# A two-layer hybrid encoder step: scores of head pairs in separate PSUM banks, layers written out, weights through 20 stages

## The reference

```
h = rms_norm(x, norm_g)
proj = h @ w_in                       # bq bf | bi bg | cq ck | cv cg | iq | ak av ik iw | aq | ag
# HGRN2, per chunk:  att = (q exp(b)) (k exp(-b))^T, causal;  o = att v + (q exp(b)) S
# retention:         att = q k^T * decay;                     o = att v + (q R) * scale
out = x + concat(ya, yb, yc) @ w_out
```

## Time and profile before

| | us |
|---|---|
| median of 3 runs | 4273.15 (4270.22 to 4276.17) |
| profiled execution | 4272.64, span 4271.0 |
| PE busy | 3742.6 (88%) |
| DVE busy | 2621.5 (61%) |
| ACT busy | 2346.7 (55%) |
| POOL busy | 991.2 (23%) |

### The profile page before, as it was taken

One profiled execution on the slowest core, in us unless ns is written; L12 is line 12 of the kernel. 1 busy time (PEld: TensorE's weight loads), 2 busy tenths in 40 slices (PEclk: granted clock), 3 DMA queues, 4 the chain that ended last, 5 costly groups with the idle time before them and its releaser, 6 DMA issues. The chain is left out here.

```text
span 4271.0 us, 57610 instructions
## 1 busy us (share of the span) xinstructions
PE 3742.6 (88%) x17620; PEld 1778.7 (42%) x17620; DVE 2621.5 (61%) x6004; ACT 2346.7 (55%) x4386; POOL 991.2 (23%) x1712
## 2 busy tenths in 40 slices
PE   3899999996788889989939999999967888899897
PEld 1555555552233333243315555555522333332433
DVE  4666666665666767566356666666656767676562
ACT  4333333333788888877343333333247888888772
POOL 0000000002643332333100000000026433323330
PEclk9899999997799899989969999999977998999899
DMA  6211111114310000010151111111142110000010
GB/s 208 69 36 35 36 34 35 37 34 113 94 43 29 20 22 20 23 33 29 39 160 51 35 35 35 35 35 35 29 122 83 45 34 10 22 30 17 29 34 36
DMA packets 168675, 202.94 MB, mean 48 GB/s; under 512 B 76592, under 2 KB 114480, under 8 KB 168304
## 3 DMA queue, kind: packets, MB, share of 16 engines
q1 hardware_dynamic: 168464, 200.53, 15.7%
HBM read 139.08 MB, written 69.88 MB: 49 GB/s over the span
## 5 line engine op out<-in xcount | busy, mean ns | idle before, releaser
L1385 ACT ACTIVATE signs<-sc,mid 128x640 bf16<-128x640 f32 (+14 forms) x720 | 975.0, 1356 | 252.5 <-POOL mid L1441 235.1
L318 PE MATMUL PJ<-w_in_hi,hTh 128*128 128x512 f16 (+2 forms) x2176 | 827.7, 380 | 28.4 <-DVE hTl L790 16.5
L319 PE MATMUL PJ<-w_in_lo,hTh 128*128 128x512 f16 (+2 forms) x2176 | 825.2, 379 | 0.0
L320 PE MATMUL PJ<-w_in_hi,hTl 128*128 128x512 f16 (+2 forms) x2176 | 824.5, 379 | 0.0
L1290 PE MATMUL PV<-pt,va_p 128*65 128x512 f32 x1088 | 582.2, 622 | 78.5 <-ACT pt L1365 71.5
L1533 DVE SCALAR_TENSOR_TENSOR sc<-rl,iwb,sc 128x512 f32<-128x512 f32 (+5 forms) x602 | 415.0, 707 | 289.2 <-ACT rl L1356 280.5
L1438 POOL TENSOR_SCALAR dlt<-cnta,stp 128x1 f32<-128x1 f32 (+1 forms) x720 | 275.6, 383 | 1136.4 <-ACT signs L1385 1134.5
L1441 POOL TENSOR_SCALAR mid<-mid,dlt,stp 128x1 f32<-128x1 f32 (+1 forms) x720 | 438.0, 608 | 75.5
L1470 DVE CUSTOM_DVE_ANT_0 junkb<-AX,mneg 128x512 bf16<-128x512 f32 (+5 forms) x720 | 412.4, 601 | 36.5 <-PE AX L1235 30.4
L1365 ACT ACTIVATE pt<-LG 128x512 f32<-128x512 f32 (+1 forms) x612 | 330.8, 555 | 138.7 <-PE LG L1275 122.5
L1356 ACT ACTIVATE rl<-AX 128x512 f32<-128x512 f32 (+5 forms) x688 | 345.7, 530 | 109.5 <-PE AX L1248 83.1
(11 more groups left out here) (250 smaller groups left out, 5622.9 us busy)
## 6 DMA issues: line engine op xcount, KB each, us to landing
w_stage<-in SPq DMA_DIRECT2D x112, 256.0 KB, 2.9
x<-out SPq DMA_DIRECT2D x32, 512.0 KB, 3.7
yt<-y_d SPq DMA_DIRECT2D x32, 512.0 KB, 3.4
xr<-out SPq DMA_DIRECT2D x32, 512.0 KB, 3.6
out<-xr SPq DMA_DIRECT2D x32, 512.0 KB, 2.6
out<-in SPq DMA_DIRECT2D x1, 8320.0 KB, 28.5
y_d<-ga SPq DMA_DIRECT2D x32, 256.0 KB, 2.0
q<-q_d SPq DMA_DIRECT2D x32, 256.0 KB, 2.9
```

The costliest lines, as they stand in the source:

```text
L318: mm(out, hTh[:, par, c, 0:T], weights(g, c, wh), start=(c == 0), stop=False)
L319: mm(out, hTh[:, par, c, 0:T], weights(g, c, wl), start=False, stop=False)
L320: last = mm(out, hTl[:, par, c, 0:T], weights(g, c, wh), start=False, stop=(c == DC - 1))
L1385: A(signs[p][0:T, 0:W], sc[u % 3][0:T, 0:W], ACT.Sign, scale=-1.0, bias=small[u % 3]["mid"][0:T, :], accum_out=small[u % 3]["cnta"][0:T, : ...
```

## The change

Five things change together.

1. The scores of a pair of heads go to two banks: HGRN2's even heads to `ATT`, odd ones to `OU`; retention's to `ATT` and `TR[0]`. The semaphore `even_heads` goes, and the heads of a pair alternate, product by product. The waits for `sh_ok` and `yb_ok`, which guard `OU`, move from behind kvi to before the scores. VectorE masks even and odd heads in separate instructions: eight for four, and two for one.
2. The loop over the layers becomes Python's, so every instruction of both halves exists twice.
3. The copy of the input goes; the first layer reads x from the input.
4. Weights come through 20 stages: the four of before, and 16 that lie in the room of the weights of groups 6 and 7 until those are made. A stage of a group that GpSimd shares is loaded again only after all eight low halves of that group. Constants are loaded behind group 0; the gains have a semaphore of their own, and VectorE clears and scales the rest after the start.
5. GpSimd makes the low halves of chunks 2, 5 and 7 of groups 2 to 6, with two instructions each, ahead of its first block's work. ScalarE's and VectorE's calls of `split_weights` are spread anew.

```
+SPARE = (6, 7)
+POOL_GROUPS, POOL_LOW = range(2, 7), (2, 5, 7)
...
+    def rows_in(l, r0, T):
+
+        return xs[l, r0:r0 + T, :] if l else xin[r0:r0 + T, :]
...
+            own = list(range(W_STAGES))
+            six, seven = (list(range(W_STAGES + DC * i, W_STAGES + DC * i + DC)) for i in range(2))
+            stage_of = six + seven + own + six[:4] + six[4:] + seven[:4] + seven[4:] + own + seven[:4] + seven[4:] + own + seven[:4] + own + own
...
+            def stage(i):
+
+                u, wd = stage_of[i], GROUPS[chunks[i][0]][1]
+                if u < W_STAGES:
+                    return wst[:, u, 0:wd]
+                g, k = SPARE[(u - W_STAGES) // DC], (u - W_STAGES) % DC
+                n0 = (DC * GOFF[GROUPS[g][0]]) // 2 + 512 * (k % (DC // 2))
+                half = wh if k < DC // 2 else wl
+                return half[:].bitcast(F32)[:, n0:n0 + wd]
+
+            def arrived(i):
+
+                return w_stage_in[stage_of[i] // 2], 16 * sum(stage_of[j] // 2 == stage_of[i] // 2 for j in range((i | 1) + 1))
+
+            def last_in(u, i):
+
+                return max((j for j in range(i) if stage_of[j] == u), default=None)
+
+            def staged_over(g):
+
+                units = range(W_STAGES + DC * SPARE.index(g), W_STAGES + DC * SPARE.index(g) + DC) if g in SPARE else ()
+                return [j for j in (last_in(u, DC * g) for u in units) if j is not None]
+
+            def low_done(i):
+
+                g, c = chunks[i]
+                return w_lo_ok[g], DC if g in POOL_GROUPS else c + 1
+
+            def on_pool(i):
+
+                return chunks[i][0] in POOL_GROUPS and chunks[i][1] in POOL_LOW
...
+                sp.dma_start(ng[:], norm_g[l, :, :]).then_inc(gains, 16)
                 for i, (g, c) in enumerate(chunks):
-                    if i >= W_STAGES:
-                        sp.wait_ge(w_lo_ok, i - W_STAGES + 1)
-                    sp.dma_start(wst[:, i % W_STAGES, 0:GROUPS[g][1]],
-                                 weights(g, c, w_in[l])).then_inc(w_stage_in[i % W_STAGES], 16)
+                    if i == DC:
+                        for d, s in ((rope[:], c_rope[:, :, :]), (causal[:], c_causal[:, :]), (dmat[:], c_dmat[:, :, :]),
+                                     (lrow[:], c_lrow[:, :, :]), (ksc[:], c_ksc[:, :, :]), (gt[:], c_gt[:, :, :]),
+                                     (bmask[:], c_bmask[:, :]), (qg[:], q_g[l, :, :]), (kg[:], k_g[l, :, :]),
+                                     (hg[:], h_g[l, :, :]), (rg[:], r_g[l, :, :])):
+                            sp.dma_start(d, s).then_inc(consts, 16)
+                    before = last_in(stage_of[i], i)
+                    if before is not None:
+                        sp.wait_ge(*low_done(before))
+                    sp.dma_start(stage(i), weights(g, c, w_in[l])).then_inc(arrived(i)[0], 16)
...
-                    for h in (0, 2, 1, 3):
-                        p, r = h // 2, slice(64 * (h % 2), 64 * (h % 2) + 64)
-                        if h == 1:
-                            last.then_inc(even_heads, 1)
-                            pe.wait_ge(even_heads, 2 * t + 1)
+                    wait(pe, sh_ok, 2 * t)
+                    wait(pe, yb_ok, 2 * t)
+                    for p in range(2):
                         for i in reversed(range(T // WIN)):
                             m = (WIN, 2 * WIN, P, P)[i]
                             q = qe if i == 0 else qw
-                            last = mm(ATT[0:m, h * P + i * WIN:h * P + (i + 1) * WIN], kt[r, p, i, 0:m],
-                                      q[r, p, i * WIN:(i + 1) * WIN], start=True, stop=True)
+                            for h in range(2):
+                                r = slice(64 * h, 64 * h + 64)
+                                last = mm((ATT, OU)[h][0:m, p * P + i * WIN:p * P + (i + 1) * WIN], kt[r, p, i, 0:m],
+                                          q[r, p, i * WIN:(i + 1) * WIN], start=True, stop=True)
                     last.then_inc(atth_ok, 1)
...
                     pe.wait_ge(k2_ok, t + 1)
-                    wait(pe, sh_ok, 2 * t)
-                    wait(pe, yb_ok, 2 * t)
...
-                    for h in (0, 2, 1, 3):
-                        p, r = h // 2, slice(64 * (h % 2), 64 * (h % 2) + 64)
-                        if h == 1:
-                            last.then_inc(even_heads, 1)
-                            pe.wait_ge(even_heads, 2 * t + 2)
-                        last = mm(ATT[0:T, h * P:h * P + T], cqkT[r, 2 + p, 0:T], cqkT[r, p, 0:T], start=True, stop=True)
+                    for p in range(2):
+                        for h in range(2):
+                            r = slice(64 * h, 64 * h + 64)
+                            last = mm((ATT, TR[0])[h][0:T, p * P:p * P + T], cqkT[r, 2 + p, 0:T], cqkT[r, p, 0:T],
+                                      start=True, stop=True)
                     last.then_inc(attr_ok, 1)
...
+                        for g2 in sorted({chunks[j][0] for j in staged_over(g)}) if c == 0 else ():
+                            act.wait_ge(w_lo_ok[g2], DC)
+                        A(weights(g, c, wh), stage(i), ACT.Copy, scale=ng[:, c:c + 1]).then_inc(w_hi_ok, 1)
...
+                def split_low(i, n):
+
+                    g, c = chunks[i]
+                    pool.wait_ge(w_hi_ok, i + 1)
+                    nc.gpsimd.tensor_scalar(stage(i), stage(i), ng[:, c:c + 1], None, ALU.mult).then_inc(w_scaled, 1)
+                    pool.wait_ge(w_scaled, n)
+                    nc.gpsimd.tensor_tensor(weights(g, c, wl), stage(i), weights(g, c, wh), ALU.subtract).then_inc(w_lo_ok[g], 1)
...
-                    attp = ATT[:].rearrange("p (h t) -> p h t", h=4)
+                    att_even, att_odd, ret_odd = (b[:, 0:2 * P].rearrange("p (h t) -> p h t", h=2) for b in (ATT, OU, TR[0]))
                     for i in range(nw):
                         m = (i + 1) * WIN
                         tw = slice(i * WIN, m)
-                        step(V.tensor_tensor(atth[0:m, :, tw], attp[0:m, :, tw], bc(causal[0:m, tw], [m, 4, WIN], 1), ALU.mult),
+                        step(V.tensor_tensor(atth[0:m, 0::2, tw], att_even[0:m, :, tw], bc(causal[0:m, tw], [m, 2, WIN], 1), ALU.mult))
+                        step(V.tensor_tensor(atth[0:m, 1::2, tw], att_odd[0:m, :, tw], bc(causal[0:m, tw], [m, 2, WIN], 1), ALU.mult),
                              *((atth_m, t + 1) if i == nw - 1 else ()))
...
-                    step(V.tensor_tensor(attr[0:T, :, 0:T], attp[0:T, :, 0:T], dmat[0:T, :, 0:T], ALU.mult), attr_m, t + 1)
+                    step(V.tensor_tensor(attr[0:T, 0::2, 0:T], att_even[0:T, :, 0:T], dmat[0:T, 0::2, 0:T], ALU.mult))
+                    step(V.tensor_tensor(attr[0:T, 1::2, 0:T], ret_odd[0:T, :, 0:T], dmat[0:T, 1::2, 0:T], ALU.mult), attr_m, t + 1)
...
                 V.memset(mhalf[:], -0.5)
-                V.memset(ones[:], 1.0)
-                V.memset(kt[:], 0.0)
-                V.memset(atth[:], 0.0)
-                V.memset(S2[:], 0.0)
-                dve.wait_ge(consts, 16 * 12)
-
-
-                V.tensor_scalar(ng[:], ng[:], W_SCALE, None, ALU.mult)
-                V.tensor_scalar(rope[:], rope[:], UNSCALE, None, ALU.mult)
-                V.tensor_scalar(hg[:], hg[:], UNSCALE / 2, None, ALU.mult)
-                V.tensor_scalar(rg[:], rg[:], UNSCALE / 2, None, ALU.mult)
                 V.tensor_copy(identh[:], ident[:])
-                V.tensor_copy(lbl[:, 0, :], lbt[:, l, :])
-                V.tensor_copy(lbl[:, 1, :], oml[:, l, :])
-                V.memset(R2[:], 0.0).then_inc(prep, 1)
+                dve.wait_ge(gains, 16)
+                V.tensor_scalar(ng[:], ng[:], W_SCALE, None, ALU.mult).then_inc(prep, 1)
                 dve.wait_ge(prep, 1)
                 x_mean_square(0)
+                V.memset(ones[:], 1.0)
+                V.memset(S2[:], 0.0)
+                V.memset(R2[:], 0.0)
                 x_low(0)
                 split_weights(0, 1)
                 hT_low(0, 0)
+                V.memset(kt[:], 0.0)
+                V.memset(atth[:], 0.0)
+                V.tensor_copy(lbl[:, 0, :], lbt[:, l, :])
+                V.tensor_copy(lbl[:, 1, :], oml[:, l, :])
+                dve.wait_ge(consts, 16 * 11)
+                V.tensor_scalar(rope[:], rope[:], UNSCALE, None, ALU.mult)
+                V.tensor_scalar(hg[:], hg[:], UNSCALE / 2, None, ALU.mult)
+                V.tensor_scalar(rg[:], rg[:], UNSCALE / 2, None, ALU.mult).then_inc(prep, 1)
+                dve.wait_ge(prep, 2)
                 split_weights(1, 3)
...
-                sp.dma_start(xs[0, :, :], xin[:, :]).then_inc(copied, 16)
-                sp.wait_ge(copied, 16)
...
-        with nc.Fori(0, DEPTH) as l:
+        for l in range(DEPTH):
```

More of the change, by code:

```diff
@@ L57 @@
 DVE_G = {"big": 1, "cqk": 2, "cvg": 3, "iq": 4, "kvi": 5, "aq": 6, "ag": 7}
-DVE_STEPS = 49
+DVE_STEPS = 54
 class Steps:
@@ L102, in sb @@
             def sb(name, shape, dt=F32):
```

(22 more changed lines are left out.)

44 lines of the change are left out of this document (17 added, 27 removed).

## The result

The kernel after takes 4123.9 us (median of 4 runs, 4120.5 to 4129.4), the kernel before 4274.3 on the same chip (4 runs, 4270.2 to 4276.2): a ratio of 0.9651, 95% interval 0.9634 to 0.9667. The forecast was 4156 with a range of 4093 to 4215, so sign and range held, and the change gave 32 us more than its likeliest sum. The narrower range that the prediction called the forecast's own, 4130 to 4185, was missed by 6 us; the wide one was widened for the rivals, and the result fell into that part. The profiled execution took 4124.8 us, with a span of 4123.0.

What follows compares the result with a forecast made beforehand. Blocks 1 to 15 of the recurrent half were bound by TensorE's instruction stream, first blocks by a chain of weight load and high and low halves. 4272.6 - 24.5 - 44 - 48 = 4156 us, range 4093 to 4215.

Steps and rivals of the forecast that it cites:

- The copy: Program start: without the input copy, x is asked for up to 25.2 us earlier, less 0.7 for a barrier: -24.5 us.
- The scores: Line 353, each block: alternating heads take 2.2 us for 3.97; net -1.6 a block, 30 full blocks: -48 us.
- the prediction's lower bound: Line 353's scores: half of all their time goes, -2.1 us a block; the other bound was -0.2.
- The retention scores: Line 371, each block: can save 0.7 us, but TensorE then waits longer for VectorE: 0; two masks add 0.2.
- The first block: First block of each layer: next block's x transposed 102 us after the load of x; -22 a layer, -44 us.
- Written-out layers: Border between layers: more semaphores at most +3.6 us, the jump back saves perhaps 2 to 4; taken as 0.
- No overlap: Rival, scores: pairs don't overlap, only the wait goes and the extra mask takes it back: 4204 us, chance 0.24.
- the first block keeps its length: Rival, first block of each layer: gains only 5 us a layer, 4190 us in all; chance 0.13.
- the 0.87 us row: Earlier profile: VectorE's 256-element product took 0.87 us beside GpSimd's cast, against 0.69 for a product twice as long.
- The slower one: Rival, scores: each of 16 row changes a block costs 0.17 us, +92 us in 34 blocks: 4296 us, chance 0.02.
- The fast case: Rival: first blocks at transfer pace (-78), scores fully parallel (-57), clock drops gone (-27): 4086 us, chance 0.12.

Runs made afterwards that it cites:

- the serial kernel: The kernel after with the HGRN2 scores issued head by head again, still in two banks with no wait between them: 4212.9 us (one run).
- the looped kernel: The kernel after with the copy of the input and the hardware loop over both layers put back: 4158.7 us (one run).

## Why the prediction was right, point by point

**The copy** (-24.5): right in mechanism and size. The start gave 24.5, and putting the copy back cost 23.2. The 0.7 us for the barrier had no row behind it; the load of x now starts 0.66 us after the last set-up instruction does (5.71).

**The scores** (-48, measured -88 in the steady stretches): the mechanism was right, the term too small in two places. First, "each matrix still needs two passes in a row; I take 2.2 us" was too cautious: the section measured 1.96, half of the 3.97 of the earlier trace rows and so close to the prediction's lower bound. The sum by the Trainium skill (TensorEngine Tiling (Array Packing), Key Properties), which lets tiles load and multiply in parallel, was -57; of the two, the trace agrees with this one. Blocks without a drop of the clock became 1.84 us shorter (51.99 to 50.15; 2.01 from the section, less some 0.2 for the second mask), in 30 blocks 55 us. Second, the drops of the clock stood only in a rival, priced there at 27 us. They went wholly: 17 blocks had taken 1.96 us more than the others, 33 us. 55 and 33 are the 88 us of the steady stretches.

The price of a 1.8 us cut, times thirty, was thus only part of its worth. The earlier trace rows already gave a clock of 0.98, and the right question was what TensorE did when it fell. The trace of before could answer it: each time, line 353's scores.

That the sum came within 32 us is in part luck. The scores and the clock gave 40 us more than forecast and the first blocks 14 less; the miss would have been larger without this.

**The retention scores** (0, with +0.2 for the mask): right, and on its reason. Put back, they made a full block 0.15 us shorter where the prediction had 0.2; with the wait for hTl gone they cost 21 us. The wait that the earlier trace rows showed at 0.47 us on the first weight load came out at 1.44 (1.2 was forecast), and TensorE's stop at 0.95 us in each block. The prediction called the growth of this wait a consequence, and did not ask for its cure. That was worth as much as the offload costs: one line moved, -28.5 us.

**The first block** (-44, measured -30): this term was too large. The forecast had the next transposes 102 us after x; they came at 108.0. Of the 16.6 us that layer 1's first block gained, 8.4 stand already at the first projection (23.2 us after x before, 14.8 now, 14.4 forecast). No run has the four stages back with the rest kept, so what the 20 stages bring by themselves is not shown. Three places of the forecast were off:

- "GpSimd's pair costs 0.61 + 1.16 or so" took the cast of the earlier trace rows for the scaling. Scaling 512 columns in f32 took 1.56 to 2.07 us. GpSimd's three pairs now take 9.7 us a group (40.37 to 50.04). The group's 9.0 came out nearly right all the same, but as GpSimd's own time and not as turns taken with VectorE.
- VectorE's stretched scans and products were not counted outside the low halves. ScalarE waits for them, group 4 begins later, and its last low half comes 56.8 us after x in place of 53.5, group 6's at 79.3 in place of 74.5.
- The last eight chunks: the addends in the text give 87.3 (74.5 + 12.8), not the 85 written, so 2.3 us were lost in adding up. Measured, the last high half ends 93.3 us after x, 14.0 behind group 6. Two by two they wait for their stages. Timeline of ScalarE:

```profile
90.11 2.60 ACT L470 ACTIVATE w_in_hi<-w_stage,ng 128x512 f16<-128x512 f32 x4 [10.88 <-DMA w_stage<-in]
...
95.28 1.33 ACT L470 ACTIVATE w_in_hi<-w_stage,ng 128x512 f16<-128x512 f32 x2 [2.57 <-DMA w_stage<-in]
98.35 1.33 ACT L470 ACTIVATE w_in_hi<-w_stage,ng 128x512 f16<-128x512 f32 x2 [1.74 <-DMA w_stage<-in]
```

From there the rest takes 14.7 us (to 114.37), less than the 16.5 allowed, and the next transposes stand 6 us late in all. The warning that "this offload can lose 3.5 us a group where low halves bind" was right in kind: without it the block takes 93.3. Two small slips in this part change nothing: the terms given for the start add up to 14.2 and not 14.4, and 99.90 + 0.19 - 30.90 is 69.2.

**Written-out layers** (0, measured -3.7): the jump back and what goes with it saved more than I took, and the loop put back cost 4.3. The eight masks took 2.0 us where 2.4 was allowed, with no wait behind them.

**The rivals.** No overlap (4204) is what the serial kernel shows: 4212.9, with the clock's drops. That the first block keeps its length (4190) is out, since each became 13 to 17 us shorter, not 5; but its two reasons, the 0.87 us row and the whole-group waits, are what took half of the possible gain. The slower one, that changing rows costs, is out: 16 changes a block, and loads still follow at 0.1 us; the gap of 0.17 us stands once, at the start of the section. The fast case (4086) had the scores and the clock right, but not the first block.

What stays open: how GpSimd's 15 us divide between VectorE's stretched instructions and GpSimd's own slowness, what the 20 stages bring alone, and why the attention half of the looped kernel was longer. That a shorter stretch of small products keeps the clock up is shown at two lengths only, 1.96 and about 3.9 us.

## What to carry to other kernels

Where products use 64 rows each and weight loads set the pace, alternate the halves product by product into two banks; the banks alone give nothing. Where the granted clock is below 1.00 in a full stream, look in the trace for what stands before each fall: here shortening that section was worth 33 us more than its own length. After cutting a stretch on the engine that binds, ask which engine now makes it wait and what that engine does first: here one copy ahead of a wait was worth 28.5 us. And price an offload with the helper's own instruction and shape, with the stretch that it causes on the engine that it relieves, and with each wait that now needs the helper's last piece.

## What the runs showed of the hardware

- Two f32 passes of 64 rows, one in either half, load and run side by side to within 10 ns: 1.96 us in place of 3.97 for 32 passes.
- GpSimd's f32 scaling of 128 x 512 by one value a partition took 1.56 to 2.07 us, where its cast of the earlier trace rows took 0.61.
- VectorE's three-operand product went from 0.69 to 1.1 us beside GpSimd, and two scans from 0.88 to 2.02.
- TensorE's clock fell in 17 of 30 full blocks with 3.97 us of small products, each time inside that section or up to 1.1 us behind it, and in 16 of 30 when as long a section ran in pairs. It fell in none when the section took 1.96 us. A block with a drop took 1.83 to 1.96 us more.
- With no wait for hTl and no offload, TensorE was busy for 600.00 of the 600 us from 200 to 800, at a granted clock of 1.00.
